# The dummy matmuls at the branch ends and in the memory attentions taken out of a one-core transformer kernel

## Chip, cores and metric

The kernel runs on one core of a Trainium2 chip. The metric is the device time of one execution in microseconds (us), as the median of several executions. TensorE (PE in the profile) has a clock with two levels, 1.2 and 2.4 GHz; the profile gives the granted level as a share of the full one (0.5 and 1.0).

## The reference

A block of two layers is followed by a second block of one layer, on 256 rows of width 2048, all in fp32. Cut to what matters here:

```python
def first_block(...):                       # DEPTH = 2
    h = x
    for l in range(DEPTH):
        xn = rms_norm(h, mix_pre_g[l])
        ...                                 # three mixers: oa, ob, oc
        mix = jnp.concatenate([oa, ob, oc], axis=-1)
        h = h + rms_norm(jnp.einsum('bsc,cd->bsd', mix, w_out[l]), mix_post_g[l])
        xa = memory_attention(rms_norm(h, x_pre_g[l]), rms_norm(mem, mem_g[l]),
                              x_wq[l], x_wkv[l], x_wo[l])
        h = h + rms_norm(xa, x_post_g[l])
        ff = swiglu(rms_norm(h, f_pre_g[l]), f_w_gu[l], f_w_down[l])
        h = h + rms_norm(ff, f_post_g[l])
    return h

def memory_attention(h, mem_n, wq, wkv, wo):  # 4 heads of 128, 256 memory rows
    q = jnp.einsum('bsd,dhe->bshe', h, wq)
    ...
    p = jax.nn.softmax(logits, axis=-1)
    o = jnp.einsum('bhsm,bmhe->bshe', p.astype(v.dtype), v)
    return jnp.einsum('bshe,hed->bsd', o, wo)
```

The second block begins with `rms_norm_2(x, norm_w) @ w_in` and goes on with a windowed attention, a state space scan and a gated sum; the change touches only its beginning.

## The kernel before

Every weight product is done in three passes. A weight is streamed in units of 128 x 4 x 512 numbers (`raw`), ScalarE rounds it to a high part (`hi`, L1256), VectorE takes the rest (`lo`, L1911), and TensorE adds high x high, high x low and low x high into a PSUM group `acc` (L732 to L734, in the other layouts L738 and L740, L747 to L750, and L790 to L792 for the last group of a branch). There are two `acc` groups, used in turn (`g.parity`), and two PSUM buffers `tp` for transposes and small products, also used in turn (`take_turn`).

Each engine works through its own written order of instructions; semaphores tie them together. For TensorE that order is the function decorated with `@block.tensor`. The places that the change touches lie between products:

- **A branch end**, five times in the program. `h` gets the normed branch output added, and the next product needs `h` normed and transposed. A product's last group (`last_product`) ends with row tile 0 first. ScalarE squares it (L1344), GpSimd makes the root (L2825, L2827), VectorE adds `y` times the root to `h` (L2001). In `raw_norm` TensorE waits for those pieces of `h` (`h_quads`), transposes them (L843; two quads of row tile 0, then two of row tile 1), ScalarE (L1311) and VectorE (L2026) split the transposed quad into `xh` and `xl`, and `unit_ready` lets the next product start when half a quad is there (`x_half`). `k` says which end: 0 after the feed-forward (once between the layers with tag "pre", once before the second block with tag "norm"), 1 after the mixers, 2 after the memory attention (each once in a layer).
- **A memory attention**, once in each of the two layers: logits from `qxT` and `kmT` (L1059), maxima and row sums on VectorE (L2380 to L2393) and exponentials on ScalarE (L1591), transposes of the weights (L1072, after the wait for `x_weights`), ScalarE's copies `xz` (L1603), the values (L1082), and a split of the result into `cqh` and `cql` (L1608, L2407), after which the output product `xo0` starts (wait for `x_split`).

At both, TensorE also runs dummy matmuls: `stay_warm(into, src, n)` issues `n` products of 128x128 by 128x512 into an `acc` group that is overwritten later; nothing reads them.

```python
def stay_warm(into, src, n):

    for _ in range(n):
        nc.tensor.matmul(acc[into][:, 0, :], src[:, 0, 0:P], src[:, 0:2, :], start=True, stop=True)

FILL_IN = {0: (6, 3, 4), 1: (1, 4, 4), 2: (3, 3, 4)}
```

`FILL_IN` gives for a branch end how many come before the transposes of row tile 0, before those of row tile 1, and behind them. A memory attention has 4 before the logits, 4, 3, 1 and 1 before the four groups of transposes, and 5 behind the values. That makes 2 x 13 + 2 x 9 + 2 x 10 + 2 x 18 = 100. Two waits stand only before dummies: in `raw_norm` for `k` = 1 and 2 that for `out_squares` (ScalarE has read the group that the dummies write), and in the memory attention that for `acc_read` of the group `xo0`.

The program also begins with 28 transposes of the identity (L915), while the first weights load. They are left as they are.

Of the kernel before, what the change touches and what calls it, by code (L numbers as in the profile page):

```python
# [14 lines left out]
P = 128  # L15
# [38 lines left out]
def plan(specs):  # L54
    groups, unit = {}, 0
    for n, (name, kchunks, width, form) in enumerate(specs):
        groups[name] = Group(name, kchunks, width, form, unit, n)
        unit += groups[name].units
    assert unit % SLOTS == 0 and len(specs) % 2 == 0
    return groups, unit  # L60
# [31 lines left out]
LG, LU = plan(LAYER)  # L92
# [207 lines left out]
def build(nc, stream, x, mem, x_cols, mem_cols, params, rows, post_g, sparams, sinks, onehot, rel, b_rows, c_pack, out,  # L300
          toep_scratch, mem_scratch, turn_scratch, map_scratch, b_scratch, u_scratch):
    ctx = ExitStack()
    with ctx:
# [5 lines left out]
        def at_offset(name, offset, shape, dt=F32):  # L309
            return nc.alloc_sbuf_tensor_at(name, shape, dt, offset=offset)  # L310

        def sb(name, shape, dt=F32):
            here = place[0]
            place[0] += (int(np.prod(shape[1:])) * 4 + 63) // 64 * 64
            assert place[0] <= nc.sbuf_usable_end - 64, (name, place[0])
            return at_offset(name, here, shape, dt)
# [7 lines left out]
        xh, xl = xhl[:, :, 0, :], xhl[:, :, 1, :]  # L324
# [44 lines left out]
        cqh = sb("cqh", [P, 4, T], F32R)  # L369
# [23 lines left out]
        h2h = at_offset("h2h", made_at + 16384, [P, 4, T], F32R)  # L393
# [51 lines left out]
        acc = [ctx.enter_context(nc.psum_tensor(f"acc{n}", [P, NT, W], F32)) for n in range(2)]  # L445
# [3 lines left out]
        def sem(name):  # L449
            return ctx.enter_context(nc.semaphore(name))  # L450
# [8 lines left out]
        acc_read = [sem(f"acc_read{n}") for n in range(2)]  # L459
# [30 lines left out]
        out_squares = sem("out_squares")  # L490
# [124 lines left out]
        def take_turn(pe, pos, turn):  # L615

            pe.wait_ge(tp_read[turn % 2], pos.n("turn2", turn // 2 + 1))
            return tp[turn % 2]
# [6 lines left out]
        def after_turn(eng, pos, turn):  # L625

            eng.wait_ge(tp_read[turn % 2], pos.n("turn2", turn // 2 + 2))
# [11 lines left out]
        def after_group(eng, pos, g):  # L639

            eng.wait_ge(acc_read[g.parity], pos.n("acc", g.turn + 2))
# [67 lines left out]
        def _(pe):  # L709
# [116 lines left out]
                return quad_ready  # L826


            def stay_warm(into, src, n):

                for _ in range(n):
                    nc.tensor.matmul(acc[into][:, 0, :], src[:, 0, 0:P], src[:, 0:2, :], start=True, stop=True)

            FILL_IN = {0: (6, 3, 4), 1: (1, 4, 4), 2: (3, 3, 4)}

            def raw_norm(pos, k, tag, turns, g):

                src = cqh if k else h2h
                before, between, behind = FILL_IN[k]

                def tile(o, q, t):
                    for c in range(4):
                        last = nc.tensor.transpose(o[:, c, t * P:(t + 1) * P],  # L843
                                                   h[:, t, (4 * q + c) * P:(4 * q + c + 1) * P], ident[:, :])
                    return last

                def quad(q):
                    o = take_turn(pe, pos, turns[f"{tag}{q}"])
                    for t in range(NT):
                        pe.wait_ge(h_quads, pos.n(24, 8 * k + 2 * q + t + 1))  # L850
                        last = tile(o, q, t)
                    last.then_inc(tp_full, 1)

                both = [take_turn(pe, pos, turns[f"{tag}{q}"]) for q in (0, 1)]
                pe.wait_ge(acc_read[g.parity], pos.n("acc", g.turn + 1))
                if k:
                    pe.wait_ge(out_squares, pos.n(15, 5 * (k - 1) + 3))
                for t in range(NT):
                    stay_warm(g.parity, src, (before, between)[t])
                    for q in (0, 1):  # L860
                        pe.wait_ge(h_quads, pos.n(24, 8 * k + 2 * t + q + 1))
                        last = tile(both[q], q, t)
                        if t == NT - 1:
                            last.then_inc(tp_full, 1)

                def unit_ready(n):
                    q = n // 2
                    if n == 0:
                        stay_warm(g.parity, src, behind)
                    if n % 2 == 0:  # L870
                        pe.wait_ge(x_half, pos.n(12, 4 * k + q + 1))
                    else:
                        after_turn(pe, pos, turns[f"{tag}{q}"])
                        if q < 2:
                            quad(q + 2)

                return unit_ready
# [26 lines left out]
            pos = Pos(None)  # L904
# [26 lines left out]
            for layer in range(L):  # L931
                pos = Pos(layer)
                ready = raw_norm(pos, 0, "pre", LTP, LG["cq"]) if layer else given_rows(pos)
                for step, *at in MIX:
                    if step == "unit":
                        g, n = at
# [20 lines left out]
                    elif step == "ix":  # L957

                        i, b = at
# [4 lines left out]
                        for hh in range(4):  # L964
                            g, half = 4 * b + hh, slice(64 * (hh % 2), 64 * (hh % 2) + 64)
                            last = nc.tensor.matmul(o[:, 2 * (hh % 2) + hh // 2, 0:P * (i + 1)],  # L966
                                                    QI[half, g // 2, i * P:(i + 1) * P], kiT[half, 0:P * (i + 1)],
                                                    start=True, stop=True)
                        last.then_inc(tp_full, 1)
                    elif step == "bL":  # L970
                        k = at[0]
                        i, hp = PAIRS[k]
# [9 lines left out]
                    elif step == "aL":  # L982
                        k = at[0]
                        i, hp = PAIRS[k]
# [11 lines left out]
                    elif step in ("aT", "bT"):  # L996
                        k = at[0]
# [3 lines left out]
                    elif step == "bV":  # L1001
                        k = at[0]
                        i, hp = PAIRS[k]
                        after_turn(pe, pos, LTP[f"bT{k}"])
                        o = take_turn(pe, pos, LTP[f"bV{k}"])
                        for hh in range(2):
                            hd = 2 * hp + hh
                            for b in range(i + 1):
                                last = nc.tensor.matmul(o[:, 0, hh * P:(hh + 1) * P], vb[:, b, hd * P:(hd + 1) * P],
                                                        lg[k % 2][:, 2 + hh, b * P:(b + 1) * P],  # L1010
                                                        start=b == 0, stop=b == i)
                        last.then_inc(tp_full, 1)
                    elif step == "aV":
                        k = at[0]
                        i, hp = PAIRS[k]
# [31 lines left out]


                ready = raw_norm(pos, 1, "xpre", LTP, LG["xq"])
                product(pos, LG["xq"], xh, xl, unit_ready=ready)  # L1050
                free = LG["xo0"]
                pe.wait_ge(acc_read[free.parity], pos.n("acc", free.turn + 1))
                stay_warm(free.parity, xl[:, 8:10, :], 4)
                after_group(pe, pos, LG["xq"])
                pe.wait_ge(memkv_loaded, pos.n(32, 32))
                for i in range(NT):
                    o = take_turn(pe, pos, LTP[f"xL{i}"])
                    for hd in range(HX):
                        last = nc.tensor.matmul(o[:, hd, :], qxT[:, hd, i * P:(i + 1) * P], kmT[:, hd, :],  # L1059
                                                start=True, stop=True)  # L1060
# [4 lines left out]
                for i in range(NT):  # L1065
                    o = take_turn(pe, pos, LTP[f"xT{i}"])
                    for m in range(2):
                        stay_warm(free.parity, xl[:, 8:10, :], 1 if i else 4 - m)
                        pe.wait_ge(x_weights, pos.n(4, 2 * i + m + 1))
                        for hd in (2 * m, 2 * m + 1):  # L1070
                            for b in range(NT):
                                last = nc.tensor.transpose(o[:, hd, b * P:(b + 1) * P], xe[i][:, hd, b * P:(b + 1) * P],  # L1072
                                                           ident[:, :])
                        if m == 0:
                            last.then_inc(x_across, 1)
                    last.then_inc(tp_full, 1)
                for i in range(NT):
# [4 lines left out]
                                last = nc.tensor.matmul(values[:, i, hd * P:(hd + 1) * P], vm[:, b, hd * P:(hd + 1) * P],  # L1082
                                                        xz[i][:, hd, b * P:(b + 1) * P], start=b == 0, stop=b == 1)
                    last.then_inc(x_values, 1)
                stay_warm(free.parity, xl[:, 8:10, :], 5)
                pe.wait_ge(x_split, pos.n(2, 2))
                branch_products(pos, 1, "xo", cqh, cql)


                ready = raw_norm(pos, 2, "fpre", LTP, LG["gate0"])  # L1090

                def across(pos, j):
# [30 lines left out]
            pos = Pos(L)  # L1123
# [8 lines left out]
            for step, *at in SMIX:  # L1132
                if step == "unit":
                    g, n = at
# [13 lines left out]
                elif step == "wL":  # L1148
                    k = at[0]
                    i, g = k // 4, k % 4  # L1150
# [10 lines left out]
                elif step == "wT":  # L1161
                    k = at[0]
# [3 lines left out]
                elif step == "wV":  # L1166
                    k = at[0]
                    i, g = k // 4, k % 4
                    after_turn(pe, pos, STP[f"wT{k}"])
                    o = take_turn(pe, pos, STP[f"wV{k}"])  # L1170
                    for n in range(2):
                        for b in range(i + 1):
                            for r in range(2):
# [3 lines left out]
                                                        start=b == 0, stop=b == i, tile_position=(0, 64 * r))  # L1177
                    last.then_inc(tp_full, 1)
                elif step == "inputs":
# [5 lines left out]
                    for j in range(4):  # L1185
                        last = nc.tensor.matmul(o[:, j, :], b_stack[:, ("re", "im").index(part), j, :], u_stack[:, j, :],
                                                start=True, stop=True)
                    last.then_inc(tp_full, 1)
                elif step == "outputs":
# [6 lines left out]
                    for n, (m, turned_) in enumerate(terms):  # L1196
                        for j in range(4):
                            last = nc.tensor.matmul(o[32 * j:32 * j + 32, 0, :], cmap[m][:, j, :], turned_[:, j, :],  # L1198
                                                    start=n == 0, stop=n == 3, tile_position=(0, 32 * j))
# [1867 lines left out]
```

## Time and profile before

| | |
|---|---|
| time, median of 3 runs | 3049.34 us (3049.19 to 3049.7) |
| the profiled execution's own time | 3050.22 us |
| its span, first to last instruction | 3048.4 us |
| TensorE matmuls | 3030.4 us busy (99%), 15718 instructions |
| VectorE | 1994.7 us busy (65%) |
| ScalarE | 1533.3 us busy (50%) |
| mean granted TensorE clock | 1.000 |
| chain of work that ended last | 90% TensorE, 5% VectorE, 2% ScalarE |

The page's span is that of the program's instructions; the time beside it also has what lies around them. A matmul's busy time overlaps its neighbour's, since they are pipelined: one of 128x512 lasts 0.39 us in the records, and in a dense stretch one starts every 0.23 us. In a timeline the distance between two starts is therefore what an instruction takes of TensorE. In "[0.20 <-DVE h L2001]" the engine was idle for 0.20 us, and VectorE's L2001 ended the wait.

### The profile page before, as it was taken

The page shows a single profiled execution, that of the slowest core. Times are in us where ns is not written, and L with a number is a line of the kernel's source. Part 1 is how long each engine was busy: PE and PEld are TensorE (multiplying, and loading weights), DVE is VectorE, ACT ScalarE, POOL GpSimd, SP SyncE. Part 2 cuts the span into 40 slices and gives each one's busy share as a digit, 9 for nine tenths or more (in the row PEclk, how much of TensorE's full clock was granted, in tenths as well). Part 3 has the DMA queues.
Part 4 walks back from the last instruction along what each step waited for, and adds up shares of the span by engine and source line. Part 5 has one row for each costly group of instructions (what it writes and reads, how often), then busy time and mean ns, then how long its engine had stood idle before and what let it go on. Part 6 is the DMA issues. An engine that isn't in the chain of part 4 may idle for free.

```text
span 3048.4 us, 43776 instructions
## 1 busy us (share of the span) xinstructions
PE 3030.4 (99%) x15718; PEld 2559.0 (84%) x15718; DVE 1994.7 (65%) x2338; ACT 1533.3 (50%) x2011; POOL 67.4 (2%) x122
## 2 busy tenths in 40 slices
PE   9999999999999999999999999999999999999999
PEld 9888888888888888888888888888888888788887
DVE  6677756555555555777856665655665677888664
ACT  6645546444444444655546455555554555444543
POOL 0000000000000000000000000000000010000000
PEclk9999999999999999999999999999999999999999
DMA  9764554655555555555554666666666555676455
GB/s 332 244 187 158 190 176 148 220 190 189 192 186 192 191 190 190 175 181 163 188 173 145 221 220 203 204 201 205 218 206 208 168 189 181 219 231 223 167 193 173
DMA packets 167929, 596.84 MB, mean 196 GB/s; under 512 B 18845, under 2 KB 26201, under 8 KB 164953
## 3 DMA queue, kind: packets, MB, share of 16 engines
q1 hardware_dynamic: 150432, 545.33, 54.7%
q10 hardware_dynamic: 14888, 36.86, 3.5%
q0 software_dynamic: 2464, 12.67, 1.3%
q8 instruction: 97, 1.59, 0.2%
q14 instruction: 48, 0.39, 0.0%
HBM read 577.99 MB, written 17.07 MB: 195 GB/s over the span
## 4 chain that ended last, share of the span: by engine, by line
PE 90%; DVE 5%; ACT 2%; DVEq 1%; issue 1%; DMA 0%; POOL 0%; ACTq 0%; POOLq 0%; SPq 0%
PE acc L732 24%; PE acc L734 24%; PE acc L733 24%; PE acc L738 3%; PE acc L747 2%; PE acc L750 2%; PE acc L749 2%; PE acc L740 2%; DVE lo L1911 1%; PE tp L803 1%; PE tp L843 0%; PE tp L966 0%; PE tp L1198 0%; PE acc L792 0%; PE acc L790 0%
## 5 line engine op out<-in xcount | busy, mean ns | idle before, releaser
L1911 DVE TENSOR_TENSOR lo<-raw,hi 128x1024 fp32r<-128x1024 f32 x1032 | 1245.5, 1215 | 807.1 <-ACT hi L1256 796.6
L1256 ACT ACTIVATE hi<-raw 128x1024 fp32r<-128x1024 f32 x1032 | 1078.9, 1050 | 1172.7 <-PE acc L734 981.2
L732 PE MATMUL acc<-hi,xhl 128*128 128x512 f32 (+2 forms) x2504 | 971.2, 388 | 3.4 <-DVE lo L1911 1.2
L734 PE MATMUL acc<-hi,xhl 128*128 128x512 f32 (+2 forms) x2504 | 963.6, 385 | 0.0
L733 PE MATMUL acc<-lo,xhl 128*128 128x512 f32 (+2 forms) x2504 | 963.1, 385 | 0.0
L732 PEld LDWEIGHTS acc<-hi,xhl 128*128 128x128 f32 x2504 | 470.4, 188 | 99.7 <-DVE lo L1911 3.6
L734 PEld LDWEIGHTS acc<-hi,xhl 128*128 128x128 f32 x2504 | 470.2, 188 | 93.6
L733 PEld LDWEIGHTS acc<-lo,xhl 128*128 128x128 f32 x2504 | 470.6, 188 | 90.3
L732 PE MATMUL acc<-hi,hTh 128*128 128x512 f32 x640 | 249.2, 389 | 0.0
L734 PE MATMUL acc<-hi,hTl 128*128 128x512 f32 x640 | 249.0, 389 | 0.0
L733 PE MATMUL acc<-lo,hTh 128*128 128x512 f32 x640 | 249.0, 389 | 0.0
L738 PE MATMUL acc<-xhl,hi 128*128 128x512 f32 x640 | 229.9, 402 | 0.0
L740 PE MATMUL acc<-xhl,lo 128*128 128x256 f32 x640 | 178.7, 279 | 0.0
L738 PEld LDWEIGHTS acc<-xhl,hi 128*128 128x128 f32 x640 | 120.2, 188 | 30.7 <-issue 3.0
L747 PE MATMUL acc<-xhl,hi 128*128 128x256 f32 x504 | 144.2, 286 | 0.8 <-DVE xhl L2026 0.5
L749 PE MATMUL acc<-xhl,hi 128*128 128x256 f32 x504 | 142.6, 283 | 0.0
L750 PE MATMUL acc<-xhl,lo 128*128 128x256 f32 x504 | 142.5, 283 | 0.0
L734 PEld LDWEIGHTS acc<-hi,hTl 128*128 128x128 f32 x640 | 120.1, 188 | 24.9
L733 PEld LDWEIGHTS acc<-lo,hTh 128*128 128x128 f32 x640 | 120.2, 188 | 24.9
L732 PEld LDWEIGHTS acc<-hi,hTh 128*128 128x128 f32 x640 | 120.1, 188 | 24.9
L740 PEld LDWEIGHTS acc<-xhl,lo 128*128 128x128 f32 x640 | 120.7, 189 | 0.1
L2445 DVE TENSOR_TENSOR y<-y,acc 128x1024 f32<-128x1024 f32 x80 | 97.7, 1221 | 29.3 <-PE acc L734 29.3
(437 smaller groups left out, 2907.4 us busy)
## 6 DMA issues: line engine op xcount, KB each, us to landing
raw<-in_stream SPq DMA_DIRECT2D x1032, 512.0 KB, 4.2
turn_scratch<-made ACTq DMA_DIRECT2D x8, 1024.0 KB, 6.7
gpost<-in_post_g POOLq DMA_DIRECT2D x6, 1024.0 KB, 5.6
rotc<-turn_scratch ACTq DMA_DIRECT2D x8, 512.0 KB, 6.5
rots<-turn_scratch ACTq DMA_DIRECT2D x8, 512.0 KB, 8.7
u_stack<-u_scratch ACTq DMA_DIRECT2D x24, 128.0 KB, 4.4
h<-in_mem ACTq DMA_DIRECT2D x2, 1024.0 KB, 7.8
xT<-in_x_cols ACTq DMA_DIRECT2D x4, 512.0 KB, 5.5
```

What stands on the lines that cost most here:

```text
L732: nc.tensor.matmul(o, ah, high, start=first, stop=False)
L733: nc.tensor.matmul(o, ah, low, start=False, stop=False)
L734: last = nc.tensor.matmul(o, al, high, start=False, stop=final)
L738: nc.tensor.matmul(a[:, 2 * b:2 * b + 2, :], wh, xhl[:, c, :, :], start=first, stop=False, skip_group_check=True)
L740: last = nc.tensor.matmul(a[:, 2 * b, :], wl, a_h[:, c, :], start=False, stop=final, skip_group_check=True)
L747: nc.tensor.matmul(o, wh, a_h[:, c, :], start=first and b % 2 == 0, stop=False, skip_group_check=True)
L749: nc.tensor.matmul(o, wh, a_l[:, c, :], start=False, stop=False, skip_group_check=True)
L750: last = nc.tensor.matmul(o, wl, a_h[:, c, :], start=False, stop=final, skip_group_check=True)
L803: last = nc.tensor.transpose(o[:, c, t * P:(t + 1) * P], src, ident[:, :])
L1256: nc.scalar.activation(hi[s][:, :, 0:w], raw[s][:, :, 0:w], ACT.Copy).then_inc(hi_done, 1)
L1911: nc.vector.tensor_tensor(lo[s][:, :, 0:w], raw[s][:, :, 0:w], hi[s][:, :, 0:w].bitcast(F32), ALU.subtract).then_inc(split_done, 1)
L2445: nc.vector.tensor_tensor(y[:, :, n * W:(n + 1) * W], y[:, :, n * W:(n + 1) * W], a[:, :, :], ALU.add).then_inc(acc_read[g.parity], 1)
```

## The change

`stay_warm`, `FILL_IN` and every call of them go, with the two waits named above. All real work, the other waits and the order on the other engines stay.

```diff
-            def stay_warm(into, src, n):
-
-                for _ in range(n):
-                    nc.tensor.matmul(acc[into][:, 0, :], src[:, 0, 0:P], src[:, 0:2, :], start=True, stop=True)
-
-            FILL_IN = {0: (6, 3, 4), 1: (1, 4, 4), 2: (3, 3, 4)}
-
             def raw_norm(pos, k, tag, turns, g):
-
-                src = cqh if k else h2h
-                before, between, behind = FILL_IN[k]
...
                 both = [take_turn(pe, pos, turns[f"{tag}{q}"]) for q in (0, 1)]
                 pe.wait_ge(acc_read[g.parity], pos.n("acc", g.turn + 1))
-                if k:
-                    pe.wait_ge(out_squares, pos.n(15, 5 * (k - 1) + 3))
                 for t in range(NT):
-                    stay_warm(g.parity, src, (before, between)[t])
                     for q in (0, 1):
...
                     q = n // 2
-                    if n == 0:
-                        stay_warm(g.parity, src, behind)
                     if n % 2 == 0:
...
                 product(pos, LG["xq"], xh, xl, unit_ready=ready)
-                free = LG["xo0"]
-                pe.wait_ge(acc_read[free.parity], pos.n("acc", free.turn + 1))
-                stay_warm(free.parity, xl[:, 8:10, :], 4)
                 after_group(pe, pos, LG["xq"])
...
                     for m in range(2):
-                        stay_warm(free.parity, xl[:, 8:10, :], 1 if i else 4 - m)
                         pe.wait_ge(x_weights, pos.n(4, 2 * i + m + 1))
...
                     last.then_inc(x_values, 1)
-                stay_warm(free.parity, xl[:, 8:10, :], 5)
                 pe.wait_ge(x_split, pos.n(2, 2))
```

## Rows read from the trace of the kernel before

**Rows 1.** The page: span, and the granted TensorE clock in 40 slices.

```profile
span 3048.4 us, 43776 instructions
...
PEclk9999999999999999999999999999999999999999
```

**Rows 2.** Groups by line, of TensorE: busy us, mean ns; idle before.

```profile
L832 PE MATMUL acc<-cqh 128*128 128x512 f32 x38 | 11.4, 410 | 0.0
L832 PE MATMUL acc<-xhl 128*128 128x512 f32 x36 | 11.2, 418 | 1.7 <-ACT xe L1591 1.7
...
L832 PE MATMUL acc<-h2h 128*128 128x512 f32 x26 | 7.3, 404 | 0.0
```

**Rows 3.** Timeline, TensorE, branch end k=1 of layer 0: start, us, instruction.

```profile
432.96 0.39 PE L792 MATMUL acc<-hi,xhl 128*128 128x512 f32 x1
...
433.59 1.32 PE L843 MATMUL tp<-ident,h 128*128 128x128 f32 x8
434.67 1.17 PE L832 MATMUL acc<-cqh 128*128 128x512 f32 x4
436.04 1.32 PE L843 MATMUL tp<-ident,h 128*128 128x128 f32 x8 [0.20 <-DVE h L2001]
437.11 1.17 PE L832 MATMUL acc<-cqh 128*128 128x512 f32 x4
438.53 0.39 PE L747 MATMUL acc<-xhl,hi 128*128 128x256 f32 x1 [0.25 <-DVE xhl L2026]
```

**Rows 4.** Timeline, VectorE, the same branch end.

```profile
435.23 1.42 DVE L2001 SCALAR_TENSOR_TENSOR h<-y,small,h 128x512 f32<-128x512 f32 x2 [0.38 <-POOL small L2827]
437.60 1.66 DVE L2026 SCALAR_TENSOR_TENSOR xhl<-tp,par,xhl 128x256 fp32r<-128x256 f32 x4 [0.96 <-ACT xhl L1311]
```

**Rows 5.** Timeline, TensorE, branch end k=0 between the layers.

```profile
1236.19 1.52 PE L832 MATMUL acc<-h2h 128*128 128x512 f32 x6
1238.04 1.32 PE L843 MATMUL tp<-ident,h 128*128 128x128 f32 x8 [0.33 <-DVE h L2001]
...
1242.81 0.50 PE L732 MATMUL acc<-hi,xhl 128*128 128x512 f32 x1 [0.34 <-DVE xhl L2026]
```

**Rows 6.** Timeline, TensorE, memory attention of layer 0.

```profile
464.68 3.72 PE L1059 MATMUL tp<-kmT,qxT 128*128 128x256 f32 x16 [0.18 <-ACT qxT L1265]
469.23 1.19 PE L832 MATMUL acc<-xhl 128*128 128x512 f32 x4 [0.83 <-ACT xe L1591]
470.25 0.60 PE L1072 MATMUL tp<-ident,xe 128*128 128x128 f32 x4
...
476.94 1.40 PE L832 MATMUL acc<-xhl 128*128 128x512 f32 x5
478.59 0.50 PE L732 MATMUL acc<-hi,cqh 128*128 128x512 f32 x1 [0.25 <-DVE cql L2407]
```

**Rows 7.** Timeline, VectorE, memory attention of layer 0.

```profile
468.78 0.69 DVE L2393 TENSOR_TENSOR xe<-xe,small 128x512 f32<-128x512 f32 x1
...
470.52 0.69 DVE L2393 TENSOR_TENSOR xe<-xe,small 128x512 f32<-128x512 f32 x1
...
477.85 0.69 DVE L2407 TENSOR_TENSOR cql<-acc,cqh 128x512 fp32r<-128x512 f32 x1 [1.10 <-ACT cqh L1608]
```

**Rows 8.** Timeline, TensorE, a gap without dummies.

```profile
2599.00 0.39 PE L734 MATMUL acc<-hi,xhl 128*128 128x512 f32 x1
2600.35 0.71 PE L1186 MATMUL tp<-u_stack,b_stack 96*128 96x256 f32 x4 [0.96 <-DVE uT L2699]
```

**Rows 9.** Windows at the end: us, busy us by engine, then PEclk, DMA, GB/s.

```profile
3045.00:3047.40 2.40, 0.00 (x0) 0.00 (x0) 0.69 (x1) 0.00 (x0) 0.00 (x0) 1.00 0.28 109
3047.40:3048.40 1.00, 0.00 (x0) 0.00 (x0) 0.00 (x0) 0.00 (x0) 0.00 (x0) 0.50 0.00 0
```

**Rows 10.** Windows, L915 alone: length, PE busy, PEld busy, PEclk, DMA, GB/s.

```profile
1.60:6.10 4.50, 4.46 (x21) 4.47 (x22) 1.00 0.86 258
6.10:7.10 1.00, 0.98 (x9) 0.74 (x7) 1.00 0.98 369
```

## Prediction

> **What bounds the kernel now.** I read the page first: in all 40 slices TensorE has its full clock, and the span is 3048.4 us [rows 1]. With TensorE 99% busy, time can go only where it does dummy work or waits, so the second view is the groups of TensorE by line. It shows the 100 dummies in three groups, 38, 36 and 26 of them, and almost no idle time before them [rows 2]. Whether they delay anything is not to be seen there. For that I went to the timelines of the stretches around them, TensorE's first, then that of the engine that releases it. Last I looked for places that show what the clock does when TensorE pauses.
>
> **The change, part by part.** First, what the dummies cost now. In a dense stretch a 128x512 matmul takes 0.23 us of TensorE, so 100 of them are 23 us of its time. That would be the gain if they stood on the path.
>
> *Branch end, k = 1.* The last product step begins at 432.96 and is done 0.23 us later. Without the dummies TensorE waits until 433.59 for the first quad of `h`, transposes eight blocks, waits from 434.67 to 436.04, transposes eight again, and waits from 437.11 to 438.53 [rows 3]. The second transposes start 0.1 us after the first half of VectorE's pair of additions, which begins at 435.23 and takes 1.42 us for two. The product starts 0.1 us after the first two of VectorE's four splits (437.60, 1.66 us for four) [rows 4]. Between the last dummy of a batch and the next real instruction lies more than a dummy's 0.23 us each time: four dummies from 437.11 are through by about 438.0, the product starts at 438.53. So the dummies end before what TensorE waits for, and removing them gains nothing. The mixers' end of layer 1 and both ends after the memory attentions have the same shape.
>
> *Branch end, k = 0, twice.* Six dummies begin at 1236.19 and take 1.4 us; the transposes start at 1238.04, 0.4 us after they are through, and the product at 1242.81 [rows 5]. Again nothing is gained.
>
> *Memory attention, twice.* Here one batch is on TensorE's own path. Four dummies begin at 469.23, and the transposes follow at 470.25 without a pause [rows 6]. VectorE had the weights ready at 468.78 + 0.69 = 469.47 [rows 7]. So those transposes can start 0.7 us sooner. But the stretch does not end there: it ends with VectorE's last split, 477.85 + 0.69 = 478.54, and the output product starts at 478.59 [rows 6, 7]. Between them lies ScalarE's row of exponentials and copies, which is in order and busy with the second row tile until the first copy can start. I cost the gain at 0; its bounds are 0 and 0.7 us for each attention, 1.4 us in all. The five dummies from 476.94 are through at 478.1, before the split.
>
> *The two waits.* Each stood ahead of dummies alone, and a later wait of the same engine ends after it. Price 0. What covers it is the wait for `h_quads` and for the logits; if that cover went, nothing would be left to wait for either, since no reader of the group is overtaken by a real write. The other engines keep their order, and no DMA is added or moved.
>
> *What the dummies hold up: the clock.* Without them TensorE is empty for 0.4 + 1.4 + 1.4 = 3.2 us of the 5.3 us at a k = 1 end [rows 3]. At a k = 0 end it is empty for 6.6 us less two batches of transposes of some 1.1 us, 4.5 us, with 1.85 us in one piece [rows 5]. In the attention, from the last logits at about 468.25 to the output product at 478.59, there are three such holes: about 1.3 us before the transposes; 1.4 us between the first batch, done at about 469.9, and the second, for which VectorE is ready at 470.52 + 0.69; and 1.65 us at the end [rows 6, 7]. What has the trace to say on such holes? Two places speak. A gap of 1.35 us between two starts, 1.1 us of it empty, stands alone in dense work, and the clock holds [rows 8]. At the end of the program TensorE has nothing after 3045.0, and at 3047.4, 2.4 us later, the granted clock is 0.5, the 1.2 GHz level, though all before it had been dense [rows 9]. So the fall can come after little more emptiness than a single hole here has, and the holes here come in groups of two and three within a few us, with less work between them than emptiness. I take it that the clock falls once in each of the seven stretches.
>
> *The price of a fall.* No fall in the middle of the program is in this trace, but its start shows the low level under unbroken work. The 28 identity transposes begin at 1.6 us. In the 4.5 us to 6.1 there are 21 of them, 0.21 us each; after 6.1 there are nine in 1.0 us, 0.11 us each [rows 10]. (The view prints 1.00 for the first stretch as well, because its first clock record is at 6.1; the spacing tells that the level was the lower one.) So the low level lasted 4.5 us under work, and cost 4.5 - 21 x 0.11 = 2.2 us. A fall at a branch end comes while TensorE still waits for part of the time, and waiting costs nothing at either level; I take 1.8 us. The bounds are 0, if all of a low stretch lies in waiting, and 2.2 us.
>
> *The transposes.* On whether the transposes in between keep the clock up, the row says they count for something: at the start nothing else had run on TensorE when the clock rose [rows 10]. The Trainium skill, "TensorE: Matmul & The Clock Gate", Part 4, says the opposite, that a transpose does not count as TensorE being busy in the way a matmul does. By that rule each branch end would be empty from its first transpose wait to its product, 5.3 us and more, and the falls at branch ends would be certain; by the row they are only likely. The sum is the same 12.6 us by both; what differs is the chance of the first rival. The trace speaks against the page at its start, so I go by the row.
>
> **The sum.** Seven falls at 1.8 us are 12.6 us, less 0 for the dummies. The profiled execution took 3050.22 us, 0.9 us more than the median of the runs, 3049.34 us. So 3062.8 us for an execution like the profiled one, and 3062 us for the median.
>
> **The rivals.**
>
> *A. The clock holds.* The transposes and small products between the holes are enough, and no single hole (1.85 us at most) is as long as the end's 2.4 us. For it: the transposes that raised the clock, and the gap that it survived. Against it: at the end a dense stretch had just run, which is not so within the holes here. Everything then stays on the other engines' path: 3049.3 us. This is the case on the other side, not slower. It decides at the point where no hand-over lets the clock fall. A rule that bears on it: the Trainium skill, same page, "Why this matters for your kernels", warns only of idle gaps longer than any that opens here. By that rule the time is this rival's. The trace partly disagrees: 2.4 us of nothing sufficed.
>
> *B. Few falls.* Only up to three of the seven stretches lose the clock, as chance puts them: 3 x 1.8 = 5.4 us, 3051 to 3055 us. For it: the k = 1 end is empty for 3.2 us only.
>
> *C. The low level stays, or comes more often.* Each attention has three holes and its own small products, which at the low level take twice as long and stand on its path; the five branch ends could fall and each lose the full price. With 11 falls (five ends, three in each attention) at 2.2 us this gives 24 us: 3073 us. For it: between the holes of an attention there is no dense product stretch of the length of the start's 4.5 us to raise the clock. Against it: logits and values are 3.7 us of TensorE work each.
>
> *D. The freed TensorE time counts.* The 0.7 us of each attention reaches the end and the clock holds: 3047.9 us. Against it: the last split on VectorE.
>
> **How the numbers follow.** Forecast (four to nine falls, 3056 to 3068 us) 0.58; A 0.16; B 0.07; C (over 3068 us) 0.17; D 0.02. A measurement of this kernel tells about 0.2% from no change, 6.1 us. Slower by more is the forecast and C: 0.75. Within it are A, B and most of D: 0.24; faster gets 0.01 for a D larger than I can price. The range goes from A's 3049 to C's 3073 us and leaves out D and the far part of C, under 1 in 10. It is not narrower, because A alone holds more than 1 in 10 and lies at its low edge. The likeliest case's own range is 3056 to 3068 us.
>
> **What would show it.** In the changed profile the granted clock should be 0.5 in a stretch beginning in or just behind each hand-over, about 433 to 439, 463 to 479, 500 to 506 and 1236 to 1243 us and the same places in layer 1. Right behind it the starts of 128x512 matmuls should stand some 0.43 us apart instead of 0.23, for a few us. Each product's first instruction should start as long after its branch's last as before, since VectorE sets it. The output product of an attention should start at the same distance from the logits where the clock holds, and later where it does not. Clock 1.0 all through with the time unchanged would be A. Clock 1.0 with a longer time would mean that something I have not seen depended on the dummies. Low stretches that last much longer than 4.5 us, or more than one in a hand-over, would be C. If low stretches are there but the time is not, TensorE was not the path behind the hand-overs, and my price for a fall is wrong.

## The result, and the profile after

The changed kernel takes 3053.5 us as the median of 22 executions (3051.1 to 3059.8), the kernel before, beside it, 3049.2 us (3048.5 to 3051.5). The ratio is 1.0016, with a 95% interval of 1.0010 to 1.0022: slower by 4.4 us, less than the 6.1 us that I had said a measurement could tell, and far from the 12.7 us forecast. With 22 executions the interval is narrower than I had thought, so the slowdown is real. It lies inside the range of 3049 to 3073 us, outside the likeliest case's 3056 to 3068 us, and it fits "few falls", the case that I gave 0.07.

The page of one profiled execution (its own time 3052.28 us) begins as follows.

```profile
span 3050.5 us, 43582 instructions
## 1 busy us (share of the span) xinstructions
PE 3010.0 (99%) x15618; PEld 2545.7 (83%) x15618; DVE 1994.0 (65%) x2338; ACT 1533.2 (50%) x2011; POOL 67.3 (2%) x122
...
PEclk9999999999999999999999999999999999999999
```

The 100 matmuls are gone (15718 before), everything else is there, and in tenths of a slice the clock looks as full as in [rows 1]. A slice is 76 us long, so this row can't show what was looked for. The windows around the hand-overs show it. Columns: stretch, its length, busy time of TensorE, granted clock, DMA share, GB/s.

```profile
434.90:438.20 3.30, 1.52 (x10) 1.00 0.00 0
438.30:441.60 3.30, 2.83 (x13) 0.50 0.01 2
469.00:472.30 3.30, 1.50 (x9) 1.00 0.38 156
472.40:475.80 3.40, 3.06 (x14) 0.50 0.02 5
1236.90:1243.90 7.00, 4.09 (x23) 1.00 0.23 75
1615.90:1619.20 3.30, 1.06 (x9) 1.00 0.19 72
1619.30:1622.60 3.30, 3.06 (x16) 0.50 0.00 0
```

There are three low stretches, at 438.3, 472.4 and 1619.3 us, each some 3.4 us long, and each right behind a few us in which TensorE was less than half busy. The k = 0 end at 1237 us, with the longest hole, kept its clock in this execution, although TensorE was busy for only 1.72 of the 3.50 us from 1236.9. So a pause of that kind goes before a low stretch but does not always bring one.

What one costs is to be read in TensorE's timeline of the k = 1 end of layer 0.

```profile
433.15 0.39 PE L792 MATMUL acc<-hi,xhl 128*128 128x512 f32 x1
433.88 1.23 PE L833 MATMUL tp<-ident,h 128*128 128x128 f32 x8 [0.34 <-DVE h L1981]
436.23 1.32 PE L833 MATMUL tp<-ident,h 128*128 128x128 f32 x8 [1.12 <-DVE h L1981]
438.77 0.55 PE L747 MATMUL acc<-xhl,hi 128*128 128x256 f32 x1 [1.22 <-issue]
439.12 0.42 PE L749 MATMUL acc<-xhl,hi 128*128 128x256 f32 x1
...
442.88 0.28 PE L750 MATMUL acc<-xhl,lo 128*128 128x256 f32 x1
443.00 1.04 PE L833 MATMUL tp<-ident,h 128*128 128x128 f32 x8
```

From the last product step to the next product it is 438.77 - 433.15 = 5.62 us; before it was 438.53 - 432.96 = 5.57 us [rows 3]. The dummies did not stand in the way, and without them the transposes wait for the same VectorE additions, with 1.12 us of idle time where 0.20 us stood. Behind the start, though, the first 24 steps of the product, up to the next transposes, take 443.00 - 438.77 = 4.23 us. Before, it was 2.99 us, from 438.53 [rows 3] to the same transposes:

```profile
441.52 1.04 PE L843 MATMUL tp<-ident,h 128*128 128x128 f32 x8
```

The stretch costs 1.24 us: TensorE is busy for 2.83 us of it, and a step of 128x256 takes 0.21 us there instead of 0.12.

At the k = 0 end nothing of the kind is there:

```profile
1238.07 0.39 PE L792 MATMUL acc<-hi,h2l 128*128 128x512 f32 x1
1240.24 1.23 PE L833 MATMUL tp<-ident,h 128*128 128x128 f32 x8 [1.78 <-DVE h L1981]
1242.33 1.32 PE L833 MATMUL tp<-ident,h 128*128 128x128 f32 x8 [0.87 <-DVE h L1981]
1244.96 0.47 PE L732 MATMUL acc<-hi,xhl 128*128 128x512 f32 x1 [1.31 <-issue]
```

6.89 us from last step to product, against 6.85 us before, whose last step began at 1235.96. The two low stretches in the attentions cost time as well. First layer 0, then layer 1:

```profile
466.15 3.72 PE L1041 MATMUL tp<-kmT,qxT 128*128 128x256 f32 x16 [1.11 <-ACT qxT L1245]
480.75 0.50 PE L732 MATMUL acc<-hi,cqh 128*128 128x512 f32 x1 [1.41 <-DVE cql L2387]
...
1612.20 3.72 PE L1041 MATMUL tp<-kmT,qxT 128*128 128x256 f32 x16 [1.11 <-ACT qxT L1245]
1627.19 0.50 PE L732 MATMUL acc<-hi,cqh 128*128 128x512 f32 x1 [1.41 <-DVE cql L2387]
```

From logits to output product the attention of layer 0 now takes 480.75 - 466.15 = 14.60 us, against 478.59 - 464.68 = 13.91 us [rows 6]; that of layer 1 takes 1627.19 - 1612.20 = 14.99 us, against 13.92 us (1609.82 to 1623.74). So 1.24 + 0.69 + 1.07 = 3.0 us lie in the three places. At the five hand-overs that held, TensorE's work stands as far behind that of before on the far side as on the near one, to 0.1 us.

The spans differ by 2.1 us. The rest came and went outside the hand-overs: TensorE stands 3.5 us later than before at 1647 us, 1.5 us later at 2600, and 2.1 us later at the end. So about 2 us were made up in the second block, where no dummy ever stood and both executions had their full clock. Single executions differ by some 2 us there, whatever the clock does. The execution of before that was profiled was itself 0.9 us over the median.

### The profile page after: what moved, and what is told of

Same layout as the page of the kernel before. It is cut to its first block, busy times and chain, and to the rows that moved or that the text cites. A ratio compares the mean times of both kernels' runs of the same rounds, so it can differ in the third digit from the quotient of the medians.

```text
span 3050.5 us, 43582 instructions
## 1 busy us (share of the span) xinstructions
PE 3010.0 (99%) x15618; PEld 2545.7 (83%) x15618; DVE 1994.0 (65%) x2338; ACT 1533.2 (50%) x2011; POOL 67.3 (2%) x122
## 4 chain that ended last, share of the span: by engine, by line
PE 90%; DVE 5%; DVEq 2%; ACT 2%; issue 1%; ACTq 0%; DMA 0%; POOL 0%; POOLq 0%; SPq 0%
PE acc L732 24%; PE acc L734 24%; PE acc L733 24%; PE acc L738 3%; PE acc L747 2%; PE acc L750 2%; PE acc L749 2%; PE acc L740 2%; DVE lo L1891 2%; PE tp L803 1%; PE tp L833 1%; PE tp L951 0%; PE tp L1178 0%; PE acc L792 0%; PE acc L791 0%
```

## Experiments

My theory after the result: the cost is nothing but time at the low clock level, and how much of it there is differs from one execution to the next, since the holes lie near what the clock bears. The rival: something else hangs on the dummies, such as a slower answer of TensorE after a pause, at a fixed price for each hand-over or dummy. Every run reports its mean granted clock, so the first can be checked in all of them.

**Which dummies.** `e1_ends` takes out those of the branch ends alone, `e2_attention` those of the memory attentions alone.

```diff
 # e1_ends, against before
-                if k:
-                    pe.wait_ge(out_squares, pos.n(15, 5 * (k - 1) + 3))
-                    stay_warm(g.parity, src, (before, between)[t])
-                    if n == 0:
-                        stay_warm(g.parity, src, behind)
 # e2_attention, against before
-                free = LG["xo0"]
-                pe.wait_ge(acc_read[free.parity], pos.n("acc", free.turn + 1))
-                stay_warm(free.parity, xl[:, 8:10, :], 4)
-                        stay_warm(free.parity, xl[:, 8:10, :], 1 if i else 4 - m)
-                stay_warm(free.parity, xl[:, 8:10, :], 5)
```

> Only the 64 dummies at the branch ends are out (with the wait for out_squares); the 36 in the memory attentions stay. Clock theory: the cost is a number of low stretches of TensorE's clock. In the profile of the changed kernel one of the three low stretches lies behind a branch end and two in memory attentions, so some runs keep a mean clock of 1.000 or 0.999, and the time is 3050 to 3051.5 us, 1 to 2.5 us over before, with low stretches only at branch ends. Rival (something else depends on the dummies, such as TensorE answering later after a pause): the cost goes by their number, 64 of 100, 2.8 us, and it is there with the clock at 1.000 too, spread evenly over the five ends.

> Only the 36 dummies in the two memory attentions are out (with the wait for acc_read). Clock theory: one or two low stretches, both inside the attentions, 1.5 to 3 us over before, 3050.5 to 3052 us; together with the run that takes out the branch ends' dummies it gives the 4.4 us of the whole change. Rival (cost by number of dummies): 36 of 100, 1.6 us, with no low stretch needed. If the transposes that start sooner were worth something, the runs with clock 1.000 would be up to 1.4 us faster than before.

Measured: `e1_ends` 3055.4 us (11 executions, 3051.8 to 3059.5; ratio 1.0018, interval 1.0009 to 1.0028), mean clock 0.995 to 0.998. `e2_attention` 3050.2 us (3049.3 to 3052.3; 1.0003, 0.9994 to 1.0012), mean clock 0.999 in all 11. Both expectations missed: `e1_ends` costs 6.2 us where 1 to 2.5 were expected, `e2_attention` 1.0 us where 1.5 to 3 were. The branch ends carry the cost, more than I had read from one profile's three stretches. It is also more than the whole change's 4.4 us, but the intervals overlap, so that alone says nothing. The profile of `e1_ends` has two low stretches of a new length, at both k = 0 ends, besides a short one at 438 us and one of 6.8 us at 1653 us. Columns as in [rows 9].

```profile
1240.50:1250.70 10.20, 8.44 (x27) 6.42 (x26) 9.48 (x14) 5.25 (x11) 0.31 (x1) 0.50 0.17 52
2390.80:2401.00 10.20, 8.35 (x27) 6.50 (x26) 9.59 (x14) 5.27 (x11) 0.20 (x1) 0.50 0.16 49
```

The first of these is the same hand-over that held in the profile above, with the same instructions. In it the product steps of 128x512 start 0.43 us apart:

```profile
1237.38 0.39 PE L792 MATMUL acc<-hi,h2l 128*128 128x512 f32 x1
...
1241.65 1.97 PE L843 MATMUL tp<-ident,h 128*128 128x128 f32 x8 [0.72 <-DVE h L1996]
1244.65 0.77 PE L732 MATMUL acc<-hi,xhl 128*128 128x512 f32 x1 [1.03 <-issue]
...
1247.35 0.63 PE L732 MATMUL acc<-hi,xhl 128*128 128x512 f32 x1
1247.77 0.63 PE L733 MATMUL acc<-lo,xhl 128*128 128x512 f32 x1
1248.20 0.63 PE L734 MATMUL acc<-hi,xhl 128*128 128x512 f32 x1
...
1249.91 1.45 PE L843 MATMUL tp<-ident,h 128*128 128x128 f32 x8
```

Here the low level began before the second transposes, and they took longer too (1.97 us instead of 1.32). The product starts 1244.65 - 1237.38 = 7.27 us after the last step, 0.42 us later than the 6.85 us of before, and its first twelve steps take 5.26 us instead of 2.86 (1242.81 to 1245.67). So this stretch of 10.2 us costs 2.8 us up to there.

`e2_attention` also answers whether the freed 0.7 us of an attention is worth anything. Its layer 0 attention ran at full clock:

```profile
464.56 3.72 PE L1056 MATMUL tp<-kmT,qxT 128*128 128x256 f32 x16 [1.11 <-ACT qxT L1260]
469.50 0.63 PE L1068 MATMUL tp<-ident,xe 128*128 128x128 f32 x4 [1.22 <-DVE xe L2388]
...
478.47 0.50 PE L732 MATMUL acc<-hi,cqh 128*128 128x512 f32 x1 [1.41 <-DVE cql L2402]
```

The first transposes start 469.50 - 464.56 = 4.94 us after the logits, where it was 5.57 us [rows 6]. The output product starts 13.91 us after the logits, exactly as before. The gain is used up on the way; VectorE's split sets the end. The one low stretch of this execution lies in the attention of layer 1, 3.4 us from 1617.2.

**Which branch ends.** `e6_k0` and `e7_k12` set rows of `FILL_IN` to zero.

```diff
-            FILL_IN = {0: (6, 3, 4), 1: (1, 4, 4), 2: (3, 3, 4)}
+            FILL_IN = {0: (0, 0, 0), 1: (1, 4, 4), 2: (3, 3, 4)}
 # and in e7_k12
+            FILL_IN = {0: (6, 3, 4), 1: (0, 0, 0), 2: (0, 0, 0)}
```

> Only the 26 dummies of the two k = 0 ends are out; all else as before, with its waits. These ends have the longest holes (4.5 us of 6.6 empty). Clock theory: they lose the clock in many executions, for up to 10 us as in the profile with all branch ends bare (3.0 us of time each); 3050 to 3055 us. If they held in nearly all executions, 3049.2 us and clock 1.000, and the cost of the bare branch ends would be in the other three.

> Only the 38 dummies of the four k = 1 and k = 2 ends are out; all else as before. Clock theory: shorter holes (3.2 to 3.5 us of 5.3 to 5.6 empty), so fewer low stretches for each end than at k = 0, 1.3 us each; 3050 to 3053 us. With the run for k = 0 it should add up to the cost of the bare branch ends, 6.2 us.

Measured: `e6_k0` 3051.3 us (3049.2 to 3052.9; 1.0005, 0.9996 to 1.0014), mean clock 0.998 or 0.999. `e7_k12` 3051.5 us (3050.7 to 3054.3; 1.0008, 0.9999 to 1.0017), mean clock 0.998 in two and 0.999 in nine. By the medians the two ends of k = 0 cost 2.3 us and the four of k = 1 and 2 cost 2.5 us, 1.2 and 0.6 us an end; by the means it is 2.0 and 2.6 us, 1.0 and 0.7 us an end. That an end with the longer holes costs more fits the clock theory, but is not shown: neither interval excludes 1. Their sum, 4.9 us, is under the expected 6.2 us of `e1_ends`, within the intervals. (The expectation of `e6_k0` speaks of "the other three" ends; they are four.) In the profile of `e6_k0` one of its two ends fell, at 1238.6 us for 10.2 us, and the other held.

**The changed kernel once more, and its two waits.** `a1_again` is the changed kernel unchanged. `e5_waits` puts the two waits back without any dummies:

```diff
+                if k:
+                    pe.wait_ge(out_squares, pos.n(15, 5 * (k - 1) + 3))
...
+                free = LG["xo0"]
+                pe.wait_ge(acc_read[free.parity], pos.n("acc", free.turn + 1))
```

> The changed kernel once more, for a second profile and beside the partial ones. Clock theory: the number of low stretches is not the kernel's alone but differs from execution to execution, so this profile has another number or other places than the three of the first (438, 472 and 1619 us), a median of 3052 to 3056 us, and each 3.4 us of low clock costs 1.1 to 1.5 us. Rival (a fixed cost of TensorE's pauses): low stretches at the same three places and the same cost in each.

> The changed kernel with its two waits put back (out_squares at the k = 1 and k = 2 ends, acc_read before the attention's logits), without dummies. Theory: they wait for nothing that a later wait does not wait for longer, so the time is the changed kernel's, about 3053.5 us with a mean clock of 0.996 to 0.999. Rival: the waits cost or save something of their own, and the time at equal clock lies off the line of 3049.2 us plus 0.31 us for each us of low clock that the runs so far give.

Measured: `a1_again` 3053.5 us (3051.5 to 3057.9; 1.0013, 1.0004 to 1.0023), mean clock 0.996 to 0.999. `e5_waits` 3053.8 us (3051.8 to 3058.2; 1.0017, 1.0008 to 1.0026), 0.995 to 0.999. The waits cost nothing that these runs can tell. The second profile of the changed kernel has other low stretches than the first, so the rival of the same places and the same cost in each falls here:

```profile
473.20:476.50 3.30, 3.04 (x14) 2.79 (x15) 1.74 (x5) 2.42 (x7) 0.00 (x0) 0.50 0.02 5
1586.00:1592.60 6.60, 5.97 (x28) 6.00 (x29) 6.60 (x13) 2.22 (x6) 0.00 (x0) 0.50 0.22 76
1623.50:1626.80 3.30, 3.20 (x16) 3.07 (x16) 0.18 (x1) 1.20 (x2) 0.00 (x0) 0.50 0.00 0
2391.50:2398.20 6.70, 4.81 (x16) 3.75 (x16) 6.15 (x10) 4.60 (x10) 0.13 (x1) 0.50 0.01 2
```

Nothing at 438 us this time, but the k = 1 end of layer 1 and the end before the second block, for 6.6 and 6.7 us. The profiled execution took 3057.0 us.

What each low stretch cost can be read by setting TensorE's instructions against the same ones in the profile of before. The numbers say how many us later they start than there.

```
near, us (of before)    after  a1_again  e1_ends
430                       0.2     2.2      -0.1
460, behind k=1           1.5     2.2       1.4
495, behind attention     2.2     2.9       1.4
1260, behind k=0          2.1     2.9       4.3
1605, behind k=1          2.4     5.6       4.3
1640, behind attention    3.5     7.1       4.3
1665, behind k=2          3.5     7.2       6.5
2405, behind k=0          3.5     8.5       9.4
2600, in second block     1.5     6.1       7.2
3040                      2.1     6.9       7.3
```

Every step at a hand-over belongs to a low stretch: those of 3.3 to 3.4 us cost 0.7 to 1.5 us (in `a1_again` 0.7 and 1.5, where 1.1 to 1.5 was expected), the longer ones 1.3 to 2.9 us. Over the eleven stretches of these three profiles it is 18.7 us for 61 us at the low level, 0.31 us for each. Where no low stretch lies, the work keeps its distance to 0.1 us, so a hand-over has no fixed price. What changes between the hand-overs, 2 us before 430 us in `a1_again` and about 2 us between 2405 and 2600 us in all three, comes at full clock and where no dummy stood.

The three profiles of kernels with no fill (`after`, `a1_again`, `e5_waits`) have low stretches at 3, 4 and 3 of the eight hand-overs. The attention of layer 0 fell in all three, the k = 2 ends and the k = 0 end between the layers in none, the others in one or two.

**Transposes in place of the dummies.** `e3_transposes`:

```diff
-                for _ in range(n):
-                    nc.tensor.matmul(acc[into][:, 0, :], src[:, 0, 0:P], src[:, 0:2, :], start=True, stop=True)
+                for _ in range(2 * n):
+                    nc.tensor.transpose(acc[into][:, 0, 0:P], ident[:, :], ident[:, :])
```

> Each dummy matmul of 128x512 becomes two transposes of the identity (0.11 us each, so about the same TensorE time). If transposes keep the clock up as matmuls do: mean clock 1.000 in every run and 3049.2 us as before. If a transpose does not count as work for the clock: low stretches as in the changed kernel or more, 3053 us or over, clock 0.998 or under.

Measured: 3049.8 us (3047.6 to 3053.3; 1.0002, 0.9993 to 1.0011), mean clock 1.000 in all 11 executions, where the kernel without fill (`after`, `a1_again`, `e5_waits`) never had it in 44. Since a single low stretch of 3.4 us makes the mean 0.999, none of the 11 had one. The times still scatter, by 5.7 us, more than those of any other kernel at that clock; why stays open. In the profile (columns as in [rows 9]; the granted clock is the third figure from the right):

```profile
433.00:438.60 5.60, 5.01 (x37) 3.82 (x36) 4.26 (x9) 4.69 (x10) 0.75 (x2) 1.00 0.02 9
1236.00:1242.80 6.80, 5.81 (x44) 4.59 (x42) 5.82 (x10) 5.78 (x12) 1.66 (x3) 1.00 0.22 77
```

A branch end that holds nothing but transposes keeps the clock. The Trainium skill, "TensorE: Matmul & The Clock Gate", Part 4, says that transposes do not count as TensorE being busy in that way. Its figures are for another type, bf16; for the fp32 transposes of this kernel the measurement decides against it.

**How many are needed.** `e4_half` issues `n // 2` in each batch (42 of 100), `e9_third` `n // 3` (26), `e8_one_batch` 28 in one batch for each hand-over. (The expectation of `e4_half` says 44; its own list adds up to 42, and its profile has 15660 matmuls, 58 fewer than before.)

```diff
 # e4_half; e9_third has n // 3
-                for _ in range(n):
+                for _ in range(n // 2):
 # e8_one_batch
-            FILL_IN = {0: (6, 3, 4), 1: (1, 4, 4), 2: (3, 3, 4)}
+            FILL_IN = {0: (0, 3, 0), 1: (0, 4, 0), 2: (0, 3, 0)}
-                stay_warm(free.parity, xl[:, 8:10, :], 4)
-                        stay_warm(free.parity, xl[:, 8:10, :], 1 if i else 4 - m)
+                        stay_warm(free.parity, xl[:, 8:10, :], 0 if i or m else 4)
-                stay_warm(free.parity, xl[:, 8:10, :], 5)
```

> Half of the dummies of every batch, rounded down (44 of 100: 3, 1, 2 / 0, 2, 2 / 1, 1, 2 at the branch ends; 2, 2, 1, 0, 0, 2 in an attention). Clock theory with a threshold of its own: the holes are shortened enough that few or no low stretches are left, clock 1.000 or 0.999, 3049 to 3050.5 us. Rival (cost by number): half of the 4.4 us, 3051.4 us.

> 28 dummies are left, one batch for each hand-over: 3 or 4 between the two transposes of a branch end, 4 before the first transposes of an attention. Clock theory: half of all dummies held the clock at 1.000 and the time at that of before, so the emptiness has a limit somewhere between; with 28 I expect clock 0.999 to 1.000 and 3049 to 3051 us. Rival (cost by number): 72 of 100 out, 3.2 us, 3052.4 us.

> 26 dummies, a third of every batch, rounded down (2, 1, 1 / 0, 1, 1 / 1, 1, 1 at the branch ends; 1, 1, 1, 0, 0, 1 in an attention), against 28 in one batch for each hand-over, which gave 3051.9 us. If only the emptiness summed over a hand-over counts: as there, 3051 to 3053 us, clock 0.998 to 0.999. If spreading them helps by itself: nearer to the half fill's 3049.0 us, clock 0.999 to 1.000.

Measured: `e4_half` 3049.0 us (3048.0 to 3050.0; 0.9999, 0.9990 to 1.0008), mean clock 1.000 in nine and 0.999 in two. `e8_one_batch` 3051.9 us (3049.6 to 3056.2; 1.0010, 1.0001 to 1.0019), 0.998 or 0.999. `e9_third` 3050.6 us (3049.6 to 3053.8; 1.0007, 0.9998 to 1.0016), 0.998 or 0.999. By the clock, 42 dummies do nearly all that the hundred do; 26 do not. The expectation of `e8_one_batch` missed: 2.9 us over before where up to 2 were expected, near the 3.2 us of the rival. But the cost does not go by the number of dummies, which would have given 2.6 us for `e4_half` and 2.8 us for `e1_ends`, where -0.1 and 6.2 us were measured. Whether spreading them helps is open: third and single batch had the same clocks, and their intervals overlap. With half of them TensorE is busy for 3.88 of 5.60 us and 4.33 of 6.80 us at these ends:

```profile
433.00:438.60 5.60, 3.88 (x22) 2.43 (x22) 4.26 (x8) 4.60 (x10) 0.75 (x2) 1.00 0.03 12
1236.00:1242.80 6.80, 4.33 (x24) 2.65 (x23) 5.70 (x9) 5.67 (x11) 1.69 (x4) 1.00 0.23 77
```

**All runs together.** The low time of an execution follows from its mean clock: 2 x (1 - clock) x span. The mean clock is given to 0.001, which is 6 us of low time, so single values are coarse and the averages better. Where all values are the same, as in `e2_attention`, the average is no better: its profiled execution had 3.6 us at the low level, not 6.1.

```
kernel          dummies  runs  mean low time, us  mean time, us
e3_transposes     100*    11         0.0             3049.9
e4_half            42     11         1.1             3048.9
e2_attention       64     11         6.1             3050.4
e7_k12             62     11         7.2             3052.0
e9_third           26     11         9.4             3051.2
e6_k0              74     11         9.4             3051.4
e8_one_batch       28     11         9.4             3052.5
a1_again            0     11        13.9             3054.1
changed kernel      0     22        16.1             3054.2
e5_waits            0     11        16.7             3054.2
e1_ends            36     11        18.9             3055.2
* as 200 transposes
```

A straight line through the 132 executions is 3049.1 us + 0.31 us for each us of low time (correlation 0.90). Its value without low time is that of the kernel before (median 3049.2 us). The 44 executions without any fill, taken alone, give 3049.7 + 0.28 us, the first uncertain by 0.7 us. So a second cost, or a gain, of a few tenths of a us is not excluded; one like the 4.4 us is.

## Why the prediction was right or wrong

- *The count of hand-overs*: the prediction counts five branch ends and seven stretches, and so does the list of places ahead of it. There are six ends, the four of k = 1 and k = 2 and the two of k = 0 (2 x 9 + 2 x 10 + 2 x 13 dummies), and eight stretches with the attentions. By its own step the sum should have been 8 x 1.8 = 14.4 us, further from what came out.
- *The dummies stand beside the path, and removing them gains nothing*: right. 5.62 us against 5.57 at the k = 1 end, 6.89 against 6.85 at k = 0, and 13.91 us on both sides in an attention at full clock, where the transposes did start sooner. Rival D is refuted by that row of `e2_attention`.
- *The two waits, price 0*: right, by `e5_waits`.
- *The cost is the clock, at the 1.2 GHz level behind the hand-overs, its steps 0.43 us apart*: right. *The product's start unchanged*: right where the low level begins as the product does (5.62 us against 5.57), but at a k = 0 end whose second transposes already ran at the low level it came 0.42 us later (7.27 us against 6.85, `e1_ends`).
- *"I take it that the clock falls once in each of the seven stretches"*: this step failed. Three fell in the first profile and four in the second, of eight, and not the same ones. I had one row of a fall, with 2.4 us of nothing behind a dense stretch [rows 9], and one of a gap that held [rows 8], and took the seven holes to lie surely on the side of the fall. They lie at the edge. The same hand-over falls in one execution of the changed kernel and holds in another (k = 1 of layer 0, k = 1 of layer 1, the end before the second block). In such a case the sum needs a chance for each hand-over, not a count. The mean low time of the changed kernel is 16 us, of which about 1 us in the first profile lies behind the last instruction of TensorE.
- *1.8 us a fall*: too high for this kernel, but the smaller part of the error. The start's 4.5 us under work at the low level [rows 10] were taken as what a fall brings. The falls of the first profile lasted 3.4 us and cost 1.24, 0.69 and 1.07 us; those of the second cost 0.7 to 2.7 us. That is 9.2 us for seven falls, 1.3 us each. The rate of 2.2 / 4.5 = 0.49 us for each low us holds only for unbroken work; over all executions it was 0.31, since TensorE waits or runs small transposes in part of a low stretch. By the averages the changed kernel has some 15 us of low time inside its work, at 0.31 us each 4.6 us. Number and price were both too high, and 4.4 us came out where 12.6 were in the sum. (In [rows 10] 21 and nine make 30 of 28 transposes: two lie in both windows. Seven begin after 6.1, and their 0.11 us stands.)
- *Rival A* (the clock holds) is wrong: no execution of the changed kernel had a mean clock of 1.000. So hand-overs without a single hole as long as the program end's 2.4 us did lose the clock: at the k = 1 end of layer 0 idle times of 0.34 and 1.12 us and most of one of 1.22 us went before the low stretch. The Trainium skill's rule on long gaps ("TensorE: Matmul & The Clock Gate", "Why this matters for your kernels") would have given this rival's 3049.3 us; the medians of the kernels without fill are 3053.5, 3053.5 and 3053.8 us. *Rival C* was right in that the low level can last much longer than 4.5 us (6.7 us in the changed kernel, 10.2 us in three others), but not in how often.
- *The transposes*: the row at the program's start was the better guide; by `e3_transposes` they keep the clock.
- *0.2% as what can be told from no change*: too coarse for 22 executions of each; 4.4 us was told.

## What to carry to other kernels

Here dummy matmuls that fit into waits cost nothing that was measured, and they held the clock. Judge them by the mean clock over several executions, and look for the smallest fill that keeps it near 1.000: here 42 of 100, with 1.000 in nine executions of eleven. When a stretch falls in one execution and holds in the next, neither one profile nor a count of holes gives the cost. Multiply the average low time by a rate that was measured: here 0.31 us for each us. Half of TensorE's busy time in a low stretch is too much as an estimate: by the windows of the first profile it gives 1.4, 1.5 and 1.5 us, where 1.24, 0.69 and 1.07 us were lost, since part of that work is not on the path. A clock row in 40 slices hides stretches of 3 to 10 us, so ask for windows around each hand-over.

## What was not expected of the hardware

- Low stretches lasted 3.4, 6.7 or 10.2 us, behind the same hand-over with the same work too: 6.7 us (`a1_again`) and 10.2 us (`e5_waits`) at the end before the second block, 6.6 and 3.4 us in the same two at the k = 1 end of layer 1. In the longest of `e1_ends` TensorE is busy for 8.44 of 10.20 us, and the level stays low.
- Whether one comes is not set by the kernel alone: mean clocks of the changed kernel ran from 0.994 to 0.999, its times from 3051.1 to 3059.8 us, where the kernel before stayed within 3048.5 and 3051.5 us. Without its dummies the kernel is less steady as well as slower. What in an execution decides it stays open; no run tried to set it.
- Transposes of fp32 kept the clock as dummy matmuls of about the same TensorE time did (1.000 in 11 of 11 executions).
